# A two-layer hybrid attention trunk: ScalarE's square roots moved ahead of its first gate activations

## The chip, the core and the metric

The kernel runs on one core of a Trainium2 chip. The metric is the device time of one execution in microseconds (us). TensorE (PE) multiplies matrices, VectorE (DVE) and ScalarE (ACT) work element by element, SyncE (SP) and GpSimd (POOL) start the transfers. Each engine works through its own queue in order; semaphores order the engines against each other. ScalarE evaluates functions from a table that it holds; where the function of an instruction is not in it, the program has an ACT_TABLE_LOAD ahead of that instruction. Copy, Identity, Square and Relu show no load here; Tanh and Sqrt each show one after the other.

## What is computed

Two layers over 256 tokens of width 1024, in float32. What matters here is the token mixer:

```python
proj = jnp.einsum('bsd,dn->bsn', h, w_in)
cq, ckv, kr, qkv_b, qkv_c, iq, ik, iw, gate_logits = split_columns(proj)
q_a = jnp.einsum('bsr,rn->bsn', rms_norm(cq, g_cq), w_uq).reshape(B, S, MLA_HEADS, MLA_QK)
kv_a = jnp.einsum('bsr,rn->bsn', rms_norm(ckv, g_ckv), w_ukv).reshape(B, S, MLA_HEADS, MLA_NOPE + MLA_V)
...
q_a = rms_norm(q_a, qn_mla).transpose(0, 2, 1, 3)
k_a = rms_norm(k_a, kn_mla).transpose(0, 2, 1, 3)
q_a = jnp.concatenate([q_a[..., :MLA_NOPE], apply_rope(q_a[..., MLA_NOPE:], pos)], axis=-1)
...
g_a, g_b, g_c = jnp.split(jax.nn.sigmoid(gate_logits), 3, axis=-1)
merged = g_a * y_a + g_b * y_b + g_c * y_c
return jnp.einsum('bsd,de->bse', merged, w_out)
```

Branch a is latent attention (8 heads of 96), branches b and c have 4 heads of 64 each with normalized q and k ("pairs"), and c has an indexer of 16 small heads. Every rms_norm needs a sum of squares, a square root and a reciprocal. Before the mixer stands a modulated rms_norm, after it a second one with a SwiGLU.

## The kernel before, in words

**Slabs.** All weights stream through a ring of three slabs, up to 128 x 2048 floats. SP loads slab n into `raw` when VectorE is done with slab n-3. ScalarE copies it rounded into `w_hi` (`hi(l, s)`, L873), VectorE subtracts to get the rest `w_lo` (`lo(l, s)`, L1174), and TensorE multiplies three times per tile (hi x hi, lo x hi, hi x lo; L479 to 481 for gate slabs, L542 to 544 for the latents' slabs). `hi` waits for its transfer and until TensorE has used slab n-3; `lo` waits for `hi`; TensorE waits for `lo`. There is no planner: each engine's order is written out by hand.

**Slabs around the change**, in TensorE's order: GATE0 and GATE0+1 (gates 0 and 1), UQ, UQ+1, UQ+2 (latents to q, 128 x 1536), UKV (latents to k and v, inside the indexer's heads), GATE1 to GATE1+5 (gates 2 to 7). A gate is a slab product in a bank of PSUM that `gate_act` (L918) turns by Tanh with scale 0.5 (sigmoid written through tanh), with a signal `gate_out`.

**ScalarE, first place** (L982 to L1028): slab UQ, squares of the latents (L992), the latents turned and scaled (L997), gate 0, slab UQ+1, squares of the c pairs (L1003), the two roots of the latents (L1009), gate 1, slab UQ+2, squares of the b pairs, the two roots of the pairs (L1017), slabs UKV and GATE1, the copies of q out of PSUM (L1026), then 16 relus of the indexer (L1046) with the squares of q (L1033), slab GATE1+1 and the copies of k and v (L1040) among them, slab GATE1+2, copies of the pairs (L1051). TensorE waits for both gates (L641) before the indexer's first score (L651, L652), since those go into the gates' banks.

**VectorE, first place**: lo of UQ, the rest of the latents (L1285), lo of UQ+1, a tile of the modulation (L1181, twice), the sums of the c pairs (L1293), the reciprocal, the rotary key (L1306 to L1313), lo of UQ+2, another tile, the sums of the b pairs, the normalization of the c pairs, lo of UKV, then the indexer's sums (L1344, L1346) behind each relu.

**Second place.** ScalarE (L1055 to L1066): squares of k, root 1 for q's heads (L1057), gate 2, slab GATE1+3, root 2 for k's heads (L1063), and gates 3 to 5, each with a slab behind it. VectorE (L1377 to L1414): lo of GATE1+2, the head sums of q (L1380), the gain on q (L1384), q's rotation (L1388 to L1393), the head sums of k (L1396, L1399), lo of GATE1+3, then the norms of q and k. The signal `mss_done` goes from the head sums to the roots, `mstd_done` back.

Of the kernel before, what the change touches and what calls it, by code (L numbers as in the profile page):

```python
# [9 lines left out]
ALU = mybir.AluOpType  # L10
ACT = mybir.ActivationFunctionType
AX_X = mybir.AxisListType.X

P = 128
# [4 lines left out]
TT = T // P  # L19
# [4 lines left out]
A_HEADS, A_NOPE, A_ROPE, A_QK, A_V = 8, 64, 32, 96, 64  # L24
# [123 lines left out]
def slab_words(s):  # L148

    if S_B <= s < S_GATE0:  # L150
        return PB
    return 2 * Q_RANK if S_UQ <= s < S_UKV else SLAB


def gate_slab_no(g):

    return S_GATE0 + g if g < 2 else S_GATE1 + g - 2


def gate_bank(g):  # L160

    return 7 - g if g < 2 else g % 3 if g < 6 else g % 2
# [32 lines left out]
def build(nc, x, c, ada, slabs, vec, gain_rows, const, out):  # L195
    with ExitStack() as ctx:
        def sb(name, shape, dt=F32):
            return ctx.enter_context(nc.sbuf_tensor(name, shape, dt))

        def event(name, per_layer):  # L200
            return Event(ctx.enter_context(nc.semaphore(name)), per_layer)
# [12 lines left out]
        acc = sb("acc", [P, 3072])  # L214
# [13 lines left out]
        eps = small[:, 0:1]  # L228
        ssc = small[:, 1:5]
        krss = small[:, 5:7]  # L230
# [8 lines left out]
        ss16b = small[:, 48:64]  # L239
# [38 lines left out]
        def gate(g):  # L278
            if g < 6:
                at = [C_IQ, 1024, C_C][g // 2]  # L280
                return proj[:, g % 2, at:at + 512]
            return own[:, (g - 6) * 512:(g - 5) * 512]
# [61 lines left out]
        msq_done = event("msq_done", 2)  # L344
        mss_done = event("mss_done", 2)
        mstd_done = event("mstd_done", 2)
# [510 lines left out]
        def _(act):  # L857
            nc.scalar.dma_start(cols[:, :, :].rearrange("p l r -> p (l r)"), vec).then_inc(vec_in.sem, 16)
            nc.scalar.dma_start(konst[:, 0:P], const[:, 0:P]).then_inc(ident_in.sem, 16)
            link = Chain(act, act_chain)  # L860
# [5 lines left out]
            def hi(l, s):  # L866

                n, w = l * NS + s, slab_words(s)
                act.wait_ge(raw_in[n % RING].sem, 16 * (n // RING + 1))
                if n >= RING:  # L870

                    act.wait_ge(slab_used.sem, n - RING + 1)
                nc.scalar.activation(w_hi[:, n % RING, 0:w], raw[:, n % RING, 0:w], ACT.Copy).then_inc(hi_ready.sem, 1)  # L873
# [44 lines left out]
            def gate_act(l, g):  # L918

                s = gate_slab_no(g)  # L920
                act.wait_ge(slab_used.sem, slab_used.at(l, s + 1))
                nc.scalar.activation(gate(g), bank[gate_bank(g)][:, :], ACT.Tanh, scale=0.5).then_inc(gate_out.sem, 1)
# [17 lines left out]
            for l in range(DEPTH):  # L940
# [55 lines left out]
                for k in range(KT):  # L996
                    nc.scalar.activation(y_hi[:, k, :], bank[k // 2][:, (k % 2) * T:(k % 2 + 1) * T], ACT.Copy,  # L997
                                         scale=cols[:, l, R_GQ + k:R_GQ + k + 1]).then_inc(cq_hi.sem, 1)
                gate_act(l, 0)
                hi(l, S_UQ + 1)  # L1000

                def pair_squares(kind, base):
# [5 lines left out]
                for m, n in ((0, Q_RANK), (1, KV_RANK)):  # L1008
                    nc.scalar.activation(ssc[:, 2 * m:2 * m + 2], ssc[:, 2 * m:2 * m + 2], ACT.Sqrt, bias=eps,  # L1009
                                         scale=1.0 / n).then_inc(cq_std.sem, 1)  # L1010
                gate_act(l, 1)
                hi(l, S_UQ + 2)
                act.wait_ge(pss_done.sem, pss_done.at(l, 1))
                pair_squares(1, C_B)
                for kind, ss in ((0, ss16), (1, ss16b)):
                    act.wait_ge(pss_done.sem, pss_done.at(l, kind + 1))
                    nc.scalar.activation(ss, ss, ACT.Sqrt, bias=eps, scale=1.0 / HD).then_inc(pstd_done.sem, 1)  # L1017
                hi(l, S_UKV)
                hi(l, S_GATE1)

                act.wait_ge(cq_rstd.sem, cq_rstd.at(l, 1))
                act.wait_ge(slab_used.sem, slab_used.at(l, S_UQ + 3))
                for t in range(TT):
                    for ch in range(2):
                        at = t * Q_RANK + 384 * ch
                        nc.scalar.activation(q_a[:, at:at + 384], bank[2 * t + ch][:, 0:384], ACT.Copy,  # L1026
                                             scale=ssc[:, t:t + 1]).then_inc(uq_out.sem, 1)
# [28 lines left out]
                                     ACT.Square).then_inc(msq_done.sem, 1)  # L1056
                nc.scalar.activation(ss16, ss16, ACT.Sqrt, bias=eps, scale=1.0 / A_QK).then_inc(mstd_done.sem, 1)  # L1057

                act.wait_ge(kr_done.sem, kr_done.at(l, 1))
                gate_act(l, 2)  # L1060
                hi(l, S_GATE1 + 3)
                act.wait_ge(mss_done.sem, mss_done.at(l, 2))
                nc.scalar.activation(ss16b, ss16b, ACT.Sqrt, bias=eps, scale=1.0 / A_QK).then_inc(mstd_done.sem, 1)  # L1063
                for g in range(3, 6):
                    gate_act(l, g)
                    hi(l, S_GATE1 + g + 1)  # L1066
                for kind in range(2):
                    act.wait_ge(mla_tp.sem, mla_tp.at(l, kind + 1))
                    for b in range(2):
                        m = A_HEADS * kind + 2 * b  # L1070
# [87 lines left out]
        def _(dve):  # L1158
            link = Chain(dve, dve_chain)
# [10 lines left out]
            def lo(l, s):  # L1170

                n, w = l * NS + s, slab_words(s)
                dve.wait_ge(hi_ready.sem, n + 1)
                nc.vector.tensor_tensor(w_lo[:, n % RING, 0:w], raw[:, n % RING, 0:w], w_hi[:, n % RING, 0:w],  # L1174
                                        ALU.subtract).then_inc(lo_ready.sem, 1)
# [58 lines left out]
            for l in range(DEPTH):  # L1234
# [131 lines left out]
                def k_rows(kind):  # L1366

                    dve.wait_ge(pair_tp.sem, pair_tp.at(l, kind + 1))
                    for e in range(2):
# [12 lines left out]
                qv = q_a.rearrange("p (m d) -> p m d", d=A_QK)  # L1382
                q4 = q_a.rearrange("p (t h d) -> p t h d", t=TT, h=A_HEADS)
                link(nc.vector.tensor_tensor(qv, qv, gains[:, 0:A_QK].unsqueeze(1).to_broadcast([P, 16, A_QK]), ALU.mult))  # L1384
                rot = q4[:, :, :, A_NOPE:A_QK]
                ra = acc[:, 1536:2048].rearrange("p (t h d) -> p t h d", t=TT, h=A_HEADS)
                rb = acc[:, 2048:2560].rearrange("p (t h d) -> p t h d", t=TT, h=A_HEADS)
# [4 lines left out]
                                             .to_broadcast([P, TT, A_HEADS, half]), ALU.mult))  # L1392
                link(nc.vector.tensor_tensor(rot, ra, rb, ALU.add))  # L1393

                dve.wait_ge(msq_done.sem, msq_done.at(l, 2))
                link(nc.vector.tensor_reduce(ss16b, acc[:, 0:1024].rearrange("p (m d) -> p m d", d=A_NOPE), AX_X,  # L1396
                                             ALU.add))
                sb3 = ss16b.rearrange("p (t h) -> p t h", t=TT)
                nc.vector.tensor_tensor(sb3, sb3, krss.unsqueeze(2).to_broadcast([P, TT, A_HEADS]), ALU.add)\  # L1399
                    .then_inc(mss_done.sem, 1)  # L1400
                lo(l, S_GATE1 + 3)
                dve.wait_ge(mstd_done.sem, mstd_done.at(l, 1))
                link(nc.vector.reciprocal(ss16, ss16))
# [15 lines left out]
                for kind in range(2):  # L1419
                    dve.wait_ge(mla_tp.sem, mla_tp.at(l, kind + 1))  # L1420
                    for b in range(2, 4):
                        m = A_HEADS * kind + 2 * b
# [234 lines left out]
```

## Time and profile before

| | us |
|---|---|
| median of 3 runs | 994.08 (994.02 to 995.42) |
| profiled execution | 991.47 |
| its span | 989.3 |
| TensorE busy | 935.7 (95%) |
| VectorE busy | 694.0 (70%) |
| ScalarE busy | 482.7 (49%) |

The span runs from the first to the last instruction that the profile shows; the profiled execution's own time has 2.2 us around it. Times in the rows are counted from the start of the span. "L922" is line 922 of the kernel; a tile's name stands without its number. In a row of a time line, the brackets give how long the engine stood idle before it and which instruction ended that. Consecutive instructions of an engine overlap by about 0.1 us in the rows, so that start plus duration may lie just behind the next start.

### The profile page before, as it was taken

To read this page: it belongs to the slowest core of one execution; us is meant where nothing else is said; L and a number is where in the kernel's file an instruction comes from. 1 tells how busy PE (TensorE), PEld (TensorE's weight loads), DVE (VectorE), ACT (ScalarE), POOL (GpSimd) and SP (SyncE) were. 2 spreads that over 40 slices of the span, in tenths; PEclk is the share of its full clock that TensorE was granted. 3 is DMA by queue.
4 is the path that set the end of the run, shared out by engine and by line. 5 is a ranking of instruction groups with operands and counts; after the bars stand their busy time and mean duration, and the time that the engine had idled before them with its cause. 6 is when DMAs were issued, how large, how long until landed. Compare 5 with 4: busy or idle time off the path is not lost.

```text
span 989.3 us, 15954 instructions
## 1 busy us (share of the span) xinstructions
PE 935.7 (95%) x6744; PEld 880.1 (89%) x6744; DVE 694.0 (70%) x1087; ACT 482.7 (49%) x654; POOL 24.4 (2%) x49
## 2 busy tenths in 40 slices
PE   8998989998998999999989998999989899999998
PEld 6787969976987999999978997898779799999998
DVE  4997889787784656666574797988878555656443
ACT  4554776455445433343463468374553454333341
POOL 1010000000000000000000000000000000000000
PEclk8999999999998999999989999999999789999999
DMA  9979633414652776767545795251454434654541
GB/s 361 384 285 373 238 114 132 171 44 171 255 213 86 256 255 216 280 237 281 181 170 183 273 327 187 92 204 45 172 211 173 171 128 171 218 207 172 178 164 43
DMA packets 29593, 198.31 MB, mean 200 GB/s; under 512 B 3282, under 2 KB 3794, under 8 KB 7507
## 3 DMA queue, kind: packets, MB, share of 16 engines
q1 hardware_dynamic: 23474, 155.22, 43.6%
q0 software_dynamic: 5760, 41.95, 11.5%
q8 instruction: 53, 0.87, 0.3%
q10 hardware_dynamic: 288, 0.14, 0.0%
q14 instruction: 18, 0.14, 0.0%
HBM read 196.24 MB, written 1.05 MB: 199 GB/s over the span
## 4 chain that ended last, share of the span: by engine, by line
PE 62%; DVE 24%; ACT 7%; issue 4%; DMA 3%; ACTq 0%; DVEq 0%
PE bank L479 16%; PE bank L481 16%; PE bank L480 16%; DVE w_lo L1174 7%; ACT w_hi L873 2%; DVE front L1181 2%; DVE score L1346 2%; DMA raw<-in_slabs_dram 2%; DVE acc L1437 2%; PE bank L506 1%; PE bank L586 1%; PE bank L585 1%; PE bank L587 1%; DVE score L1364 1%; ACT acc L1083 1%
## 5 line engine op out<-in xcount | busy, mean ns | idle before, releaser
L1174 DVE TENSOR_TENSOR w_lo<-raw,w_hi 128x2048 fp32r<-128x2048 f32 (+2 forms) x146 | 314.6, 2160 | 138.7 <-ACT w_hi L873 137.1
L479 PE MATMUL bank<-h_hi,w_hi 128*128 128x256 f32 x1216 | 350.8, 289 | 12.1 <-DVE w_lo L1174 6.2
L873 ACT ACTIVATE w_hi<-raw 128x2048 fp32r<-128x2048 f32 (+2 forms) x146 | 262.9, 1806 | 175.0 <-PE bank L481 120.9
L481 PE MATMUL bank<-h_hi,w_lo 128*128 128x256 f32 x1216 | 347.2, 286 | 0.0
L480 PE MATMUL bank<-h_lo,w_hi 128*128 128x256 f32 x1216 | 347.2, 285 | 0.0
L479 PEld LDWEIGHTS bank<-h_hi,w_hi 128*128 128x128 f32 x1216 | 236.5, 194 | 16.7 <-issue 14.9
L480 PEld LDWEIGHTS bank<-h_lo,w_hi 128*128 128x128 f32 x1216 | 236.5, 195 | 0.1
L481 PEld LDWEIGHTS bank<-h_hi,w_lo 128*128 128x128 f32 x1216 | 236.4, 194 | 0.0
L479 PE MATMUL bank<-y_hi,w_hi 128*128 128x256 f32 x480 | 135.6, 282 | 2.2 <-DVE w_lo L1174 2.2
L480 PE MATMUL bank<-y_lo,w_hi 128*128 128x256 f32 x480 | 135.1, 282 | 0.0
L481 PE MATMUL bank<-y_hi,w_lo 128*128 128x256 f32 x480 | 135.0, 281 | 0.0
L479 PEld LDWEIGHTS bank<-y_hi,w_hi 128*128 128x128 f32 x480 | 90.4, 188 | 2.9 <-DVE w_lo L1174 2.6
L1181 DVE CUSTOM_DVE_ANT_0 front<-front,cond,cols 128x1024 f32<-128x1024 f32 x72 | 89.5, 1280 | 4.2 <-DMA front<-in_ada_dram 4.2
L480 PEld LDWEIGHTS bank<-y_lo,w_hi 128*128 128x128 f32 x480 | 90.4, 188 | 0.0
L481 PEld LDWEIGHTS bank<-y_hi,w_lo 128*128 128x128 f32 x480 | 90.3, 188 | 0.0
L1132 ACT ACTIVATE proj<-bank 128x512 f32<-128x512 f32 x22 | 13.1, 595 | 87.2 <-PE bank L481 87.2
L1083 ACT ACTIVATE acc<-acc,small 128x128 f32<-128x128 f32 x64 | 28.6, 449 | 45.1 <-DVE small L1441 45.0
L1528 DVE TENSOR_TENSOR proj<-proj,bank 128x512 f32<-128x512 f32 x22 | 15.1, 687 | 50.5 <-ACT proj L1132 50.5
L585 PE MATMUL bank<-w_hi,h_hi 128*128 128x512 f32 x112 | 43.9, 392 | 1.9 <-DVE h_lo L1222 1.9
L587 PE MATMUL bank<-w_lo,h_hi 128*128 128x512 f32 x112 | 43.6, 390 | 0.0
L586 PE MATMUL bank<-w_hi,h_lo 128*128 128x512 f32 x112 | 43.6, 389 | 0.0
L437 POOL DMA_DIRECT2D front<-in_ada_dram x31 | 16.5, 534 | 746.5 <-DVE mod L1181 464.2
(171 smaller groups left out, 1151.2 us busy)
## 6 DMA issues: line engine op xcount, KB each, us to landing
raw<-in_slabs_dram SPq DMA_DIRECT2D x124, 1024.0 KB, 5.1
front<-in_ada_dram POOLq DMA_DIRECT2D x31, 1024.0 KB, 5.7
acc<-in_ada_dram POOLq DMA_DIRECT2D x9, 1024.0 KB, 5.7
raw<-in_slabs_dram SPq DMA_DIRECT2D x16, 552.0 KB, 4.9
front<-in_ada_dram SPq DMA_DIRECT2D x5, 1024.0 KB, 11.4
raw<-in_slabs_dram SPq DMA_DIRECT2D x6, 768.0 KB, 6.7
proj<-in_ada_dram SPq DMA_DIRECT2D x2, 1024.0 KB, 9.1
x_t<-in_x_dram SPq DMA_DIRECT2D x2, 512.0 KB, 5.3
```

The costliest lines, as they stand in the source:

```text
L479: nc.tensor.matmul(b_out, st_hi, mv_hi, start=start, stop=False, skip_group_check=True)
L480: nc.tensor.matmul(b_out, st_hi, mv_lo, start=False, stop=False, skip_group_check=True)
L481: return nc.tensor.matmul(b_out, st_lo, mv_hi, start=False, stop=stop, skip_group_check=True)
L585: nc.tensor.matmul(o, hh, wh, start=False, stop=False)
L586: nc.tensor.matmul(o, hl, wh, start=False, stop=False)
L587: last = nc.tensor.matmul(o, hh, wl, start=False, stop=(k == KT - 1))
L873: nc.scalar.activation(w_hi[:, n % RING, 0:w], raw[:, n % RING, 0:w], ACT.Copy).then_inc(hi_ready.sem, 1)
L1083: nc.scalar.activation(p_sb[n % 4][:, c0:c1], p_sb[n % 4][:, c0:c1], ACT.Exp, bias=negmax[n % 2][:, t:t + 1], scale=slope, accum_out=rowsu ...
L1174: nc.vector.tensor_tensor(w_lo[:, n % RING, 0:w], raw[:, n % RING, 0:w], w_hi[:, n % RING, 0:w], ALU.subtract).then_inc(lo_ready.sem, 1)
L1181: ins = nc.vector.tensor_tensor_reduce(w, w, cond[:], 1.0, cols[:, l, col:col + 1], ALU.mult, ALU.add, mod[:, l, col:col + 1])
L1346: ins = nc.vector.scalar_tensor_tensor(out=score[:, c0:c1], in0=relu_b[h % 4][:, c0:c1], scalar=wt, in1=score[:, c0:c1], op0=ALU.mult, op1 ...
L1437: nc.vector.tensor_tensor_reduce(p_sb[n % 4][:, c0:c1], bank[4 + n % 2][:, c0:c1], mask[:, c0:c1], 1.0, NEG, ALU.add, ALU.max, rowmax[n % ...
```

## The change

ScalarE does gates 0 and 1 only behind the roots of the latents and of the pairs, between slabs UKV and GATE1, and root 2 of the latent branch's heads ahead of gate 2. For that, VectorE makes the head sums of k ahead of q's rotation and not behind it. No instruction of arithmetic is added or removed; table loads are placed by the program's build ahead of what needs them.

```diff
@@ ScalarE
                     nc.scalar.activation(y_hi[:, k, :], bank[k // 2][:, (k % 2) * T:(k % 2 + 1) * T], ACT.Copy,
                                          scale=cols[:, l, R_GQ + k:R_GQ + k + 1]).then_inc(cq_hi.sem, 1)
-                gate_act(l, 0)
                 hi(l, S_UQ + 1)
...
                     nc.scalar.activation(ssc[:, 2 * m:2 * m + 2], ssc[:, 2 * m:2 * m + 2], ACT.Sqrt, bias=eps,
                                          scale=1.0 / n).then_inc(cq_std.sem, 1)
-                gate_act(l, 1)
                 hi(l, S_UQ + 2)
...
                     nc.scalar.activation(ss, ss, ACT.Sqrt, bias=eps, scale=1.0 / HD).then_inc(pstd_done.sem, 1)
                 hi(l, S_UKV)
+                gate_act(l, 0)
+                gate_act(l, 1)
                 hi(l, S_GATE1)
...
                 nc.scalar.activation(ss16, ss16, ACT.Sqrt, bias=eps, scale=1.0 / A_QK).then_inc(mstd_done.sem, 1)
 
+                act.wait_ge(mss_done.sem, mss_done.at(l, 2))
+                nc.scalar.activation(ss16b, ss16b, ACT.Sqrt, bias=eps, scale=1.0 / A_QK).then_inc(mstd_done.sem, 1)
                 act.wait_ge(kr_done.sem, kr_done.at(l, 1))
                 gate_act(l, 2)
                 hi(l, S_GATE1 + 3)
-                act.wait_ge(mss_done.sem, mss_done.at(l, 2))
-                nc.scalar.activation(ss16b, ss16b, ACT.Sqrt, bias=eps, scale=1.0 / A_QK).then_inc(mstd_done.sem, 1)
                 for g in range(3, 6):
@@ VectorE
                 link(nc.vector.tensor_tensor(qv, qv, gains[:, 0:A_QK].unsqueeze(1).to_broadcast([P, 16, A_QK]), ALU.mult))
+                dve.wait_ge(msq_done.sem, msq_done.at(l, 2))
+                link(nc.vector.tensor_reduce(ss16b, acc[:, 0:1024].rearrange("p (m d) -> p m d", d=A_NOPE), AX_X,
+                                             ALU.add))
+                sb3 = ss16b.rearrange("p (t h) -> p t h", t=TT)
+                nc.vector.tensor_tensor(sb3, sb3, krss.unsqueeze(2).to_broadcast([P, TT, A_HEADS]), ALU.add)\
+                    .then_inc(mss_done.sem, 1)
                 rot = q4[:, :, :, A_NOPE:A_QK]
...
                 link(nc.vector.tensor_tensor(rot, ra, rb, ALU.add))
 
-                dve.wait_ge(msq_done.sem, msq_done.at(l, 2))
-                link(nc.vector.tensor_reduce(ss16b, acc[:, 0:1024].rearrange("p (m d) -> p m d", d=A_NOPE), AX_X,
-                                             ALU.add))
-                sb3 = ss16b.rearrange("p (t h) -> p t h", t=TT)
-                nc.vector.tensor_tensor(sb3, sb3, krss.unsqueeze(2).to_broadcast([P, TT, A_HEADS]), ALU.add)\
-                    .then_inc(mss_done.sem, 1)
                 lo(l, S_GATE1 + 3)
```

## Rows read from the trace of the kernel before

**Rows 1.** The page, busy time of an engine, share of the span, instructions.

```profile
PE 935.7 (95%) x6744; PEld 880.1 (89%) x6744; DVE 694.0 (70%) x1087; ACT 482.7 (49%) x654; POOL 24.4 (2%) x49
```

**Rows 2.** ScalarE's groups by form: line, operation, count, busy us, mean ns, idle before.

```profile
L922 ACT ACT_TABLE_LOAD x8 | 10.3, 1283 | 0.1
...
L1009 ACT ACT_TABLE_LOAD x2 | 2.6, 1283 | 0.0
L1017 ACT ACT_TABLE_LOAD x2 | 2.6, 1283 | 0.0
L1063 ACT ACT_TABLE_LOAD x2 | 2.6, 1283 | 0.0
```

**Rows 3.** TensorE's time line at its stalls: start, us, instruction, idle before and releaser.

```profile
97.19 0.36 PE L479 MATMUL bank<-h_hi,w_hi 128*128 128x256 f32 x1 [3.23 <-DVE w_lo L1174]
...
131.39 0.49 PE L651 MATMUL bank<-ikz,front 128*128 128x128 f32 x2 [2.77 <-ACT acc L1046]
...
168.13 0.39 PE L479 MATMUL bank<-h_hi,w_hi 128*128 128x256 f32 x1 [0.53 <-DVE w_lo L1174]
...
496.01 0.39 PE L479 MATMUL bank<-y_hi,w_hi 128*128 128x256 f32 x1 [1.72 <-DVE w_lo L1174]
...
650.40 0.39 PE L479 MATMUL bank<-h_hi,w_hi 128*128 128x256 f32 x1 [0.52 <-DVE w_lo L1174]
```

**Rows 4.** ScalarE's time line at the first place, layer 0.

```profile
106.45 3.03 ACT L997 ACTIVATE y_hi<-bank,cols 128x256 fp32r<-128x256 f32 x8 [2.98 <-PE bank L631]
109.50 1.28 ACT L922 ACT_TABLE_LOAD   x1
...
111.29 1.48 ACT L873 ACTIVATE w_hi<-raw 128x1536 fp32r<-128x1536 f32 x1
...
125.02 0.31 ACT L1017 ACTIVATE small<-small 128x16 f32<-128x16 f32 x1 [3.66 <-DVE small L1293]
125.23 3.69 ACT L873 ACTIVATE w_hi<-raw 128x2048 fp32r<-128x2048 f32 x2
128.84 1.97 ACT L1026 ACTIVATE front<-bank,small 128x384 f32<-128x384 f32 x4
```

**Rows 5.** VectorE's time line at the first place, layer 0.

```profile
99.37 2.29 DVE L1174 TENSOR_TENSOR w_lo<-raw,w_hi 128x2048 fp32r<-128x2048 f32 x1
...
107.33 3.23 DVE L1285 SCALAR_TENSOR_TENSOR y_lo<-bank,cols,y_hi 128x256 fp32r<-128x256 f32 x8 [1.58 <-ACT y_hi L997]
112.80 1.76 DVE L1174 TENSOR_TENSOR w_lo<-raw,w_hi 128x1536 fp32r<-128x1536 f32 x1 [2.25 <-ACT w_hi L873]
...
136.06 3.30 DVE L1346 SCALAR_TENSOR_TENSOR score<-acc,proj,score 128x128 f32<-128x128 f32 x8 [1.58 <-ACT acc L1046]
```

**Rows 6.** Windows: length, busy time by engine, TensorE's granted clock, DMA share, GB/s.

```profile
98.30:101.70 3.40, 3.40 (x18) 3.40 (x17) 3.40 (x4) 3.40 (x7) 0.53 (x1) 0.50 0.76 244
136.10:168.10 32.00, 30.16 (x216) 27.84 (x214) 30.63 (x47) 16.96 (x26) 0.00 (x0) 1.00 0.29 99
```

**Rows 7.** ScalarE's time line at the second place, layer 0.

```profile
161.68 0.29 ACT L1057 ACTIVATE small<-small 128x16 f32<-128x16 f32 x1
...
163.28 0.60 ACT L922 ACTIVATE proj<-bank 128x512 f32<-128x512 f32 x1
163.77 1.91 ACT L873 ACTIVATE w_hi<-raw 128x2048 fp32r<-128x2048 f32 x1
```

**Rows 8.** VectorE's time line at the second place, layer 0.

```profile
162.32 0.69 DVE L1388 TENSOR_TENSOR acc<-front,konst 128x512 f32<-128x512 f32 x1
...
164.44 1.22 DVE L1396 TENSOR_REDUCE small<-acc 128x16 f32<-128x1024 f32 x1
165.69 0.17 DVE L1399 TENSOR_TENSOR small<-small 128x16 f32<-128x16 f32 x1
165.79 2.28 DVE L1174 TENSOR_TENSOR w_lo<-raw,w_hi 128x2048 fp32r<-128x2048 f32 x1
```

**Rows 9.** The page's DMA issues: queue, count, KB each, median us to landing.

```profile
raw<-in_slabs_dram SPq DMA_DIRECT2D x6, 768.0 KB, 6.7
```

## The prediction, made before the change was run

> **What bounds the kernel now.** I read the page first: TensorE is busy 95% of the span, VectorE 70%, ScalarE 49% [rows 1]. So ScalarE's busy time as such is free, and what counts is where another engine stands still behind it. Next the groups of ScalarE by form, for the table loads: 8 ahead of the tanh of `gate_act` (L922), 2 each ahead of the roots of L1009, L1017 and L1063, each 1283 ns [rows 2]. That is 7 a layer in the part that the change touches (the 7 others, of line 864, lie outside). Then the time lines of ScalarE, VectorE and TensorE around the two places of the diff, in layer 0. Layer 1 runs the same pattern 482.27 us later (650.40 less 168.13 [rows 3]), so each term counts twice.
>
> *First place, 106 to 136 us.* ScalarE turns the latents (L997) until 109.48, loads a table, takes gate 0, and begins the high part of slab UQ+1 at 111.29 [rows 4]. VectorE has long finished its own part (107.33 + 3.23 = 110.56) and waits 2.25 us for that slab, until 112.80 [rows 5]. From there its queue is full until the sums of the second pair, for which ScalarE waits 3.66 us, until 125.02 [rows 4]. After that ScalarE is the late one: root, two slabs (125.23), the four copies of line 1026 (128.84), the first relus; TensorE waits 2.77 us for the first relu, until 131.39 [rows 3, 4], and VectorE takes up the indexer's sums 4 to 7 at 136.06, again behind ScalarE [rows 5].
>
> *Second place, 136 to 190 us.* VectorE is busy 30.63 of 32.00 us from 136.1 to 168.1 [rows 6], its gaps are those between chained instructions, and TensorE waits 0.53 us for its low part of slab GATE1+3, until 168.13 [rows 3]. So whatever delays VectorE's queue before 168.13 delays TensorE there by the same, and whatever comes early on TensorE or ScalarE gains nothing. ScalarE has its high part of that slab ready early: 163.77 + 1.91 = 165.68 [rows 7], against VectorE's start at 165.79 [rows 8]. That is 0.1 us of cover, and the change spends it.
>
> **The change, first place (gates 0 and 1 moved behind the pair roots).** Removed ahead of UQ+1: a load and a tanh. The slab begins at 109.38 (it overlaps the end of L997 by the 0.1 us that a slab overlaps any ScalarE predecessor [rows 4]) and not at 111.29: 1.91 us earlier. VectorE is free at 110.56 and the slab is ready at 110.86, so VectorE gains 1.91 - about 110.9 for 112.80. The roots of the latents need no load any more, nor do the pair roots, since the table of roots is still in place. UQ+2 begins behind UQ+1 (1.48 - 0.1), the squares (1.05) and the two roots (0.48), at 112.3. Its data are asked for when VectorE is done with the slab three before, at 99.37 + 2.29 = 101.66 [rows 5], and such a load takes 6.7 us [rows 9]: there at 108.4, in time. VectorE's queue holds nothing else that waits, so the pair sums end 1.91 earlier too, and the last pair root starts at 125.02 - 1.91 = 123.11.
>
> Added behind slab UKV and ahead of slab GATE1: one load (1.28, and 0.1 of overlap lost as the load waits for the slab to end), gate 0 and gate 1 at about 0.5 each as they overlap (0.60 alone). That is 2.40 with the gaps of 0.01 to 0.02. Queued behind it on ScalarE are GATE1, the copies of line 1026 and the first relus, and for these both other engines stand still. So the copies begin at 128.84 - 1.91 + 2.40 = 129.33: **0.5 us later**. TensorE's first score now also waits for both gates, until 127.6; that is 1.7 before it would matter. The term is +0.5 a layer. The relus, VectorE's sums and its whole full queue up to 168 shift with it, so it is not given back.
>
> **Second place.** VectorE makes the second head sum before the rotation. Its sum of 1.22 and addition of 0.17 now start at 162.32, where the rotation did, and end at 162.32 + (165.69 - 164.44) + 0.17 = 163.74 [rows 8]; the squares that they need are there (ScalarE's root behind them starts at 161.68 [rows 7]). The rotation follows and ends at 165.8 as the whole did. The work is the same, so this alone costs nothing. On ScalarE, root 1 now needs a load, since the tanh of gates 0 and 1 came before it: 161.68 + 1.30 + 0.3 = 163.3, still ahead of 163.8, hidden with 0.5 us to spare. Root 2 waits for the sum, 163.82 to 164.13. Then come the load (1.28) and gate 2, at 165.44 and not at 163.28: 2.16 later [rows 7]. Slab GATE1+3 is queued behind gate 2 and ends at 165.68 + 2.16 = 167.84. VectorE is ready for it at 165.79 and starts at 167.87. So VectorE waits **2.1 us** where it waited for nothing, and TensorE gets the slab at 170.2, not 168.13. The two loads that disappear behind this point (L1063's and the next of L922) lay after the slab and hid behind gate slabs on TensorE; their removal gives nothing. Later TensorE runs without a stall until the scores, so the 2.1 is not made up.
>
> Table loads per layer: 7 become 3 (gate 0, root 1, gate 2), 10.3 us of ScalarE in all, and none of it from the chain except the 1.91 above.
>
> **The clock.** TensorE's stall at 168.13 grows from 0.53 to 2.6 us. The stalls of 3.23 and 2.77 us [rows 3] were each followed by 3.4 us at a granted clock of 0.50, that is 1.2 GHz and not 2.4, the first of the two in [rows 6]; the one of 1.72 us at 496.01 [rows 3] was not. A new 2.6 lies between them. At half clock 3.4 us of slab work loses 1.7 us, and here TensorE is what everybody waits for. Bounds 0 and 1.7 a layer. Nearest in size is 2.77, but there the engine also had only short matmuls around the stall, so I take 0.7, a little under half.
>
> **The sum.** (0.5 + 2.1 + 0.7) x 2 = 6.6 us. The profiled execution took 991.47 (span 989.3), the median of the runs is 994.08: 998.1 for a profiled execution like that one, **1000.6 for the median**. Without any fall of the clock it would be 999.3, with one in each layer 1002.7.
>
> **A rule on the other side.** The rows show a switch of tables as 1.30 us, load to activation. The Trainium skill ("ScalarE: Activation LUTs", Table sets: the hidden batching unit) says to batch activations by set, all of one set before switching, which is just what this change does; a reader of the rule alone would expect a gain. The same page (What ACT_TABLE_LOAD costs) counts another 1.38 us of drain with each load, 2.66 in all. By that price root 1 would come after the sum and add some 0.9 a layer, an estimate from the page; no row here shows the drain.
>
> **Rivals.** (1) *The batching pays.* If the two gates at their new place are covered, because TensorE or VectorE and not ScalarE decides when line 1026 begins, and if slab GATE1+3 is not waited for, then what is left is the 1.91 a layer that VectorE gets early: 994.1 - 3.8 = 990.3. It decides from 0.5 us on: the gates must hide that much of their 2.40. Against it: ScalarE has no gap from 125.02 through the relus, and TensorE waits for it. (2) *The second wait is hidden.* If VectorE's rotation is slower in its new place, or slab GATE1+3 comes before gate 2's tanh could hold it up, only the first term is left: 995.1. Against it: one queue, in order. (3) *The clock falls in both layers*: 1002.7. (4) *The low clock of 132 to 136 goes*, as the first scores now run later and break the stall in two. It lost 1.7 a layer on TensorE, but VectorE's queue is full there; if TensorE did decide, 999.3 - 3.4 = 995.9. (5) *It doesn't do what it says*: the loads stay 7 a layer, ScalarE would be slower still, about 1002.
>
> **Chances.** Forecast with 0 to one fall of the clock 0.63, (3) 0.19, (5) 0.02, (2) and (4) together 0.09, (1) 0.07. The range runs from just over (4) to just over (3): 996.0 to 1003.2; outside lie (1), (2) and the edges. About 0.2% (2.0 us) is what a measurement of this kernel tells from no change: slower by more 0.85, within 0.08, faster 0.07.
>
> **What would show it.** Right: 13 table loads in all, for 21; VectorE's low part of UQ+1 at about 110.9; line 1026 at 129.3; a new idle of about 2 us of VectorE ahead of a low part, ended by ScalarE, near 168; TensorE's stall there 2.6. Wrong at the first term: TensorE's stall at 131 doesn't move. Wrong at the second: slab GATE1+3's high part ends before VectorE's rotation. Wrong in size: clock falls of another number than one.

## The result, and the profile of the changed kernel

The changed kernel takes 998.97 us (median of 18 runs), the kernel before 994.00 in the same comparison (18 runs): a ratio of 1.0051, 95% interval 1.0036 to 1.0066, or +5.1 us (3.6 to 6.6). The forecast was +6.6, and +5.2 without its term for the clock. Single runs of one kernel differ by several us, so below the sizes are read from distances inside one trace, and the ratios only say whether these carry through to the end.

The page of the changed kernel and its table loads (line, operation, count, busy us, mean ns, idle before):

```profile
PE 940.2 (94%) x6744; PEld 883.9 (89%) x6744; DVE 693.9 (70%) x1087; ACT 472.5 (47%) x646; POOL 24.3 (2%) x49
```

```profile
L922 ACT ACT_TABLE_LOAD x4 | 5.1, 1283 | 0.1
L1057 ACT ACT_TABLE_LOAD x2 | 2.6, 1283 | 0.0
```

ScalarE is busy 10.2 us less than in [rows 1]: 6 loads in this part and not 14 [rows 2]. The kernel is slower all the same.

ScalarE's time line in the changed kernel, layer 0, first and second place:

```profile
107.07 3.02 ACT L997 ACTIVATE y_hi<-bank,cols 128x256 fp32r<-128x256 f32 x8 [3.95 <-PE bank L631]
109.94 1.54 ACT L873 ACTIVATE w_hi<-raw 128x1536 fp32r<-128x1536 f32 x1
...
123.72 0.31 ACT L1015 ACTIVATE small<-small 128x16 f32<-128x16 f32 x1 [5.63 <-DVE small L1293]
123.94 1.90 ACT L873 ACTIVATE w_hi<-raw 128x2048 fp32r<-128x2048 f32 x1
125.86 1.28 ACT L922 ACT_TABLE_LOAD   x1
127.15 1.09 ACT L922 ACTIVATE proj<-bank 128x512 f32<-128x512 f32 x2
128.12 1.91 ACT L873 ACTIVATE w_hi<-raw 128x2048 fp32r<-128x2048 f32 x1
129.92 2.00 ACT L1026 ACTIVATE front<-bank,small 128x384 f32<-128x384 f32 x4
...
162.90 1.28 ACT L1057 ACT_TABLE_LOAD   x1
164.20 0.31 ACT L1057 ACTIVATE small<-small 128x16 f32<-128x16 f32 x1
164.88 0.31 ACT L1060 ACTIVATE small<-small 128x16 f32<-128x16 f32 x1 [0.38 <-DVE small L1389]
165.21 1.28 ACT L922 ACT_TABLE_LOAD   x1
166.51 0.60 ACT L922 ACTIVATE proj<-bank 128x512 f32<-128x512 f32 x1
167.00 1.91 ACT L873 ACTIVATE w_hi<-raw 128x2048 fp32r<-128x2048 f32 x1
```

From the end of line 997 (107.07 + 3.02 = 110.09) to line 1026 it is 19.83 us, against 128.84 - 109.48 = 19.36 in [rows 4]: +0.47. ScalarE now waits 5.63 us for the second pair sums where it waited 3.66; the gates stand behind that wait, where nothing hides them. At the second place root 1 has its load, root 2 waits 0.38 for VectorE, and gate 2 and the slab come behind it.

VectorE and TensorE behind it, at the second place; the first row is that of the head sums of q in the kernel before, the others are of the changed kernel:

```profile
158.87 1.75 DVE L1380 TENSOR_REDUCE small<-acc 128x16 f32<-128x1536 f32 x1
```

```profile
159.98 1.75 DVE L1380 TENSOR_REDUCE small<-acc 128x16 f32<-128x1536 f32 x1
...
169.01 2.29 DVE L1174 TENSOR_TENSOR w_lo<-raw,w_hi 128x2048 fp32r<-128x2048 f32 x1 [2.16 <-ACT w_hi L873]
```

```profile
171.36 0.39 PE L479 MATMUL bank<-h_hi,w_hi 128*128 128x256 f32 x1 [1.04 <-DVE w_lo L1174]
```

The row of 165.79 in [rows 8] had no idle time; here VectorE waits 2.16 us. From the head sums of q to that low part it is 169.01 - 159.98 = 9.03 us, against 165.79 - 158.87 = 6.92 before: +2.11. TensorE gets the slab 3.23 later than the 168.13 of [rows 3], 0.61 of which was already there at line 997. Its own stall is 1.04 and not the 2.6 forecast, for it was late itself. These are its two stalls ahead of that, and its stall ahead of the first scores in layer 1; then two windows, one behind the second of these stalls and one over the first scores of layer 1 (length, busy times by engine, granted clock, DMA share, GB/s):

```profile
128.29 0.38 PE L651 MATMUL bank<-ikz,front 128*128 128x128 f32 x1 [2.84 <-ACT proj L922]
...
149.48 0.33 PE L661 MATMUL bank<-konst,proj 128*128 128x128 f32 x1 [2.47 <-ACT acc L1046]
...
615.29 0.58 PE L651 MATMUL bank<-ikz,front 128*128 128x128 f32 x1 [3.60 <-ACT proj L922]
```

```profile
150.30:153.50 3.20, 3.20 (x17) 3.20 (x16) 2.90 (x7) 2.01 (x3) 0.00 (x0) 0.50 0.38 100
614.50:621.10 6.60, 5.81 (x19) 5.09 (x20) 2.77 (x6) 5.96 (x11) 0.00 (x0) 0.50 0.44 159
```

The second of these stalls, ahead of the transposes of the pairs, was in the kernel before:

```profile
148.37 0.33 PE L661 MATMUL bank<-konst,proj 128*128 128x128 f32 x1 [1.07 <-ACT acc L1046]
```

The first scores wait for the gates (the releaser is the tanh, L922). The low clock (0.50, 1.2 GHz) that lay at 132.4 to 135.8 has moved: in layer 0 a stretch of 3.4 us begins at 129.7, behind the stall and over the short matmuls of the first scores, and a second one at 150.2, in gate slab GATE1, where VectorE's coming wait of 2.16 us leaves TensorE time to lose it in. In layer 1 the stretch over the first scores lasts 6.8 us (614.4 to 621.2), the relus wait for the scores, and the fifth relu comes late (idle of VectorE before its sums 4 to 7 2.32, against 1.58 in [rows 5]):

```profile
624.89 1.20 DVE L1346 SCALAR_TENSOR_TENSOR score<-acc,proj,score 128x128 f32<-128x128 f32 x3 [2.32 <-ACT acc L1046]
```

That is +0.74 us in this layer. Summed from the trace: layer 0 0.47 + 2.11, layer 1 0.46 + 0.74 + 2.11, together 5.9 us. The profiled execution took 999.65 (span 997.5) against 991.47 (span 989.3); the other 2.3 us lie outside the two places, in stretches of low clock and in the time of layer 0's line 997, and differ from run to run.

### The profile page after: what moved, and what is told of

Read it like the earlier page. It is cut to its first block, busy times and chain, and to the rows that moved or that the text cites. A ratio compares the mean times of both kernels' runs of the same rounds, so it can differ in the third digit from the quotient of the medians.

```text
span 997.5 us, 15948 instructions
## 1 busy us (share of the span) xinstructions
PE 940.2 (94%) x6744; PEld 883.9 (89%) x6744; DVE 693.9 (70%) x1087; ACT 472.5 (47%) x646; POOL 24.3 (2%) x49
## 4 chain that ended last, share of the span: by engine, by line
PE 58%; DVE 25%; ACT 8%; issue 4%; DMA 3%; ACTq 0%; DVEq 0%
PE bank L479 16%; PE bank L481 16%; PE bank L480 16%; DVE w_lo L1174 7%; DVE front L1181 3%; ACT w_hi L873 3%; DMA raw<-in_slabs_dram 3%; DVE score L1346 2%; DVE acc L1437 2%; PE bank L585 1%; PE bank L587 1%; PE bank L586 1%; PE bank L506 1%; DVE score L1364 1%; ACT acc L1083 1%
```

## The experiments

The distances given below are taken in each trace for layer 0 / layer 1: A, from the end of line 997 to line 1026; B, VectorE's idle ahead of the low part of GATE1+3. Before: A 19.36 / 19.36, B 0 / 0. The change: A 19.83 / 19.82, B 2.16 / 2.15. A ratio is the time over that of the kernel before, with its 95% interval; 0.0010 of it is 1.0 us.

**The first place alone.**

```diff
-                gate_act(l, 0)
                 hi(l, S_UQ + 1)
...
-                gate_act(l, 1)
                 hi(l, S_UQ + 2)
...
                 hi(l, S_UKV)
+                gate_act(l, 0)
+                gate_act(l, 1)
                 hi(l, S_GATE1)
```

> The first place of the change alone: gates 0 and 1 behind the pair roots, root 2 left behind slab GATE1+3. Queue theory (ScalarE's order decides, the wait is passed on at full length): +0.5 us a layer at the first place, since the gates' 2.4 outweigh the 1.9 that VectorE gains; and at the second place root 1 now needs a table load, so that slab GATE1+3 ends 1.3 late against 0.1 of cover: VectorE waits 1.2 ahead of that slab's low part. In all +1.7 a layer, +3.4 us over before. Rival (batching pays: 5 loads a layer and not 7 take time off): faster than before, by up to 3.8. Rival (only the clock counts): as the change itself, +5, with new stretches of low clock.

Measured: ratio 1.0050 (1.0027 to 1.0074), A 19.81 / 19.82, B 1.26 / 1.27. Its time lines at the second place:

```profile
162.11 1.28 ACT L1057 ACT_TABLE_LOAD   x1
163.41 0.31 ACT L1057 ACTIVATE small<-small 128x16 f32<-128x16 f32 x1
163.73 1.28 ACT L922 ACT_TABLE_LOAD   x1
165.03 0.60 ACT L922 ACTIVATE proj<-bank 128x512 f32<-128x512 f32 x1
165.52 1.90 ACT L873 ACTIVATE w_hi<-raw 128x2048 fp32r<-128x2048 f32 x1
```

```profile
167.46 2.29 DVE L1174 TENSOR_TENSOR w_lo<-raw,w_hi 128x2048 fp32r<-128x2048 f32 x1 [1.26 <-ACT w_hi L873]
```

Moving the gates leaves the tanh table in place at root 1, and the load that this brings, some 37 us further on, is passed to VectorE in full. Both distances are as the queue has it; batching saved two loads a layer and no time. The ratio holds the expected 1.0034 inside its interval. The clock did here what it does in layer 0 of the change: TensorE waits 2.83 us for the gates ahead of the first scores, stalls 2.54 / 2.67 us ahead of the pairs' transposes, and low clock lies from 149.2 and from 637.3, 3.4 us each. So this goes with the gates' new place and not with the second place.

**The second place alone.**

```diff
                 nc.scalar.activation(ss16, ss16, ACT.Sqrt, bias=eps, scale=1.0 / A_QK).then_inc(mstd_done.sem, 1)
 
+                act.wait_ge(mss_done.sem, mss_done.at(l, 2))
+                nc.scalar.activation(ss16b, ss16b, ACT.Sqrt, bias=eps, scale=1.0 / A_QK).then_inc(mstd_done.sem, 1)
                 act.wait_ge(kr_done.sem, kr_done.at(l, 1))
                 gate_act(l, 2)
                 hi(l, S_GATE1 + 3)
-                act.wait_ge(mss_done.sem, mss_done.at(l, 2))
-                nc.scalar.activation(ss16b, ss16b, ACT.Sqrt, bias=eps, scale=1.0 / A_QK).then_inc(mstd_done.sem, 1)
```

(with VectorE's head sums of k ahead of the rotation, as in the change)

> The second place alone: VectorE's head sums of k ahead of the rotation, root 2 ahead of gate 2; gates 0 and 1 as in the kernel before. Queue theory: root 2 waits for the sum until 163.8, so gate 2 and slab GATE1+3 come 2.1 us late and VectorE waits 2.1: +4.2 us for two layers, with 5 loads a layer. The two parts don't add (3.4 + 4.2 against 5.1 measured for both), because the load ahead of root 1 that costs 1.2 when alone hides behind the wait for the sum. Rival (batching pays): no slower than before. Rival (the sum ahead of the rotation itself costs VectorE time): VectorE's instructions longer, its idle ahead of the slab unchanged.

Measured: ratio 1.0055 (1.0034 to 1.0077), A 19.36 / 19.36, B 2.15 / 2.15. VectorE's row, TensorE's two rows, and a window behind each of these stalls:

```profile
170.79 2.29 DVE L1174 TENSOR_TENSOR w_lo<-raw,w_hi 128x2048 fp32r<-128x2048 f32 x1 [2.15 <-ACT w_hi L873]
```

```profile
173.13 0.39 PE L479 MATMUL bank<-h_hi,w_hi 128*128 128x256 f32 x1 [2.64 <-DVE w_lo L1174]
...
659.69 0.39 PE L479 MATMUL bank<-h_hi,w_hi 128*128 128x256 f32 x1 [2.63 <-DVE w_lo L1174]
```

```profile
660.50:663.70 3.20, 3.20 (x17) 3.20 (x16) 3.13 (x4) 1.31 (x1) 0.00 (x0) 0.50 0.93 310
173.20:176.60 3.40, 3.40 (x29) 3.40 (x30) 3.30 (x5) 2.06 (x2) 0.00 (x0) 1.00 0.76 222
```

With TensorE on time, its stall is the 2.6 us of the forecast. Of two such stalls one was followed by 1.2 GHz (0.50) and one was not (1.00). Where it was, from the low part of the slab to the attention scores it took 24.68 us and not 23.34: 1.3 us. That was the forecast's third term, in the kernel for which it holds. Each part alone has a ratio that can't be told from that of the whole change. By the distances they are 1.8 us a layer (0.46 at the first place, and the low part 1.34 later behind the head sums of q) and 2.1, and together 2.6: they don't add, since the load ahead of root 1 hides behind root 2's wait once both are in. In this run's trace the end of line 997 in layer 0 is at 112.39 and not at 109.48: 2.9 us of its time lie ahead of anything that was edited, where the matmuls of line 506, from 10.5 us on, came every 0.21 us and not every 0.11 as before, which is half the rate. So this execution's own time overstates the edit.

**Gates 0 and 1 where ScalarE has nothing to do.**

```diff
                 for kind, ss in ((0, ss16), (1, ss16b)):
+                    if kind == 1:
+                        gate_act(l, 0)
+                        gate_act(l, 1)
+                        table(ACT.Sqrt)
                     act.wait_ge(pss_done.sem, pss_done.at(l, kind + 1))
```

(the two gates taken out ahead of UQ+1 and UQ+2; the rest as in the kernel before)

> The kernel before with gates 0 and 1 between the two pair roots, where ScalarE waits for the second sums (5.6 us in the changed kernel), and the table of roots loaded again behind them; second place as before, loads 5 a layer plus one. Queue theory: the 1.9 us that VectorE gains at slab UQ+1 stay, and the gates are covered by ScalarE's own idle time: line 1026 begins 1.9 us earlier than in before, and -1.9 a layer, -3.8 us in all, about 990.2. Root 1 has its table, so nothing changes at the second place. Rival (clock): the stall of TensorE ahead of the first relu stays near 2.8, its fall of the clock too, same as before within 1 us. Rival (TensorE becomes the bound once ScalarE is early): -1 us or less.

Measured: ratio 0.9974 (0.9951 to 0.9998), A 17.50 / 17.50, B 0 / 0. ScalarE's time line:

```profile
117.43 1.28 ACT L922 ACT_TABLE_LOAD   x1
118.72 1.09 ACT L922 ACTIVATE proj<-bank 128x512 f32<-128x512 f32 x2
119.83 1.28 ACT L864 ACT_TABLE_LOAD   x1
121.12 0.20 ACT L864 ACTIVATE small<-small 128x1 f32<-128x1 f32 x1
123.10 0.31 ACT L1019 ACTIVATE small<-small 128x16 f32<-128x16 f32 x1 [1.77 <-DVE small L1295]
...
126.92 1.97 ACT L1028 ACTIVATE front<-bank,small 128x384 f32<-128x384 f32 x4
```

(L1019 is the roots' line here, L1028 is line 1026 of the kernel before.) Two loads and two gates stand in the idle time, of which 1.77 us are left, and A is 1.86 shorter than before in each layer. So the gain that the first edit set free was real; the gates' new place had taken it back. The expected 0.9962 lies inside the interval, and the interval ends just below 1: that the kernel is faster is shown, but only just.

**The change with slab GATE1+3 first.**

```diff
+                hi(l, S_GATE1 + 3)
                 act.wait_ge(mss_done.sem, mss_done.at(l, 2))
                 nc.scalar.activation(ss16b, ss16b, ACT.Sqrt, bias=eps, scale=1.0 / A_QK).then_inc(mstd_done.sem, 1)
                 act.wait_ge(kr_done.sem, kr_done.at(l, 1))
                 gate_act(l, 2)
-                hi(l, S_GATE1 + 3)
```

> The whole change, but slab GATE1+3 goes ahead of root 2 and gate 2 on ScalarE; 3 loads a layer as in the change. Queue theory: the slab is ready at 165.2 to 165.7 on the old time line, VectorE no longer waits for it, gate 2 comes at about 167.4, still ahead of TensorE's need of its bank at 168.1. The second term goes, the first (0.5 a layer) stays: +1.0 us over before, about 995. Rival (the sum's new place on VectorE costs): stays at +4 or more. Rival (gate 2 is now too late for gate 5): TensorE stalls for a tanh near 168 by up to 1 us a layer.

Measured: ratio 1.0035 (1.0004 to 1.0066), A 19.83 / 19.82, B 0 / 0. VectorE's low part of GATE1+3, and a window in GATE1's slab in layer 0:

```profile
167.17 2.29 DVE L1174 TENSOR_TENSOR w_lo<-raw,w_hi 128x2048 fp32r<-128x2048 f32 x1
```

```profile
150.60:154.00 3.40, 3.40 (x18) 3.40 (x17) 3.09 (x8) 2.00 (x3) 0.00 (x0) 0.50 0.50 145
```

The second term is gone and the sum's new place costs VectorE nothing: from the head sums of q to the low part it is 6.91 us. The low clock of layer 0 again fell into GATE1's slab (150.6 to 154.0), and now there was no wait to lose it in: from the low part of GATE1+3 to the attention scores it took 24.02 us in layer 0, against 23.33 in layer 1, where no such stretch lay. In layer 1 the first scores wait for the gates as in the change (3.59 us), but the low clock behind that stall lasts 3.4 us and not 6.8, and the fifth relu is not late (1.59). The ratio is above the expected 1.0010, with an interval that still holds it.

**Both places mended.** The edits of the last two experiments together.

> Both places mended: gates 0 and 1 between the two pair roots (table of roots loaded again behind them), VectorE's head sums of k ahead of the rotation, and slab GATE1+3 ahead of root 2 and gate 2. 3 table loads a layer: gate 0, pair root, gate 2. Queue theory: as the kernel with the gates in the gap, which has 5 loads a layer: line 1026 begins 17.5 us behind the end of line 997 (19.36 in before), no wait ahead of the low part of GATE1+3; -3.8 us over before, and nothing more for the 4 loads fewer. Rival (loads have a price of their own): another 5.2 us less than the kernel with 5 loads.

Measured: ratio 0.9965 (0.9947 to 0.9982), A 17.50 / 17.51, B 0 / 0. Its loads, and then those of the kernel with the gates in the gap:

```profile
L864 ACT ACT_TABLE_LOAD x9 | 11.5, 1283 | 1.8 <-PEq L1642 1.6
L922 ACT ACT_TABLE_LOAD x4 | 5.1, 1283 | 0.1
```

```profile
L864 ACT ACT_TABLE_LOAD x9 | 11.5, 1283 | 1.8 <-PEq L1642 1.6
L922 ACT ACT_TABLE_LOAD x6 | 7.7, 1283 | 0.1
L1065 ACT ACT_TABLE_LOAD x2 | 2.6, 1283 | 0.0
```

Four loads fewer, 5.1 us of ScalarE, and the distances are the same; the ratios agree within their intervals, and a price of 5.2 us for the four loads would have taken the ratio below this interval. 989.7 us is the lowest median of this study, though the times don't tell it from the kernel with the gates in the gap. Line 1026 comes 1.86 us a layer earlier, 3.7 in all, which is 0.9963 and so as much as the measured gain.

**A load behind or ahead of the slab.** The first try was one line, `table(ACT.Silu)`, behind root 2 and then ahead of gate 2.

> The kernel before with one more load a layer, of a table that nothing uses (1.28, with a tiny activation some 1.5 us), between root 2 and gate 3, behind slab GATE1+3. Queue theory: 0.0, as ScalarE is some 2.4 us early there (slab GATE1+4 is ready at 171.0, VectorE takes it at 173.4). Rival (each load costs time wherever it stands): +3.0 us.

> The kernel before with the same additional load a layer, but ahead of gate 2 and so of slab GATE1+3. Queue theory: the slab is late by 1.5 less 0.1 of cover: VectorE's idle ahead of its low part 1.4, +2.8 us for two layers. Together with the run that has it behind the slab: same load, other place. Rival (load priced by number): the same for both.

Measured: ratios 1.0005 (0.9984 to 1.0027) and 1.0005 (0.9985 to 1.0024). The dose was not given. The load that Silu brought serves the tanh behind it too, and it replaced that load. With it ahead of gate 2, one activation of 0.20 us was all that was added (21 loads, as before), and the low part of GATE1+3 came 7.08 us behind the head sums of q and not 6.92: 0.16 of the 0.20 us is passed on. With it behind root 2 there are 23 loads, but the additional one a layer stands elsewhere than meant: the exponential of the attention scores, which needs no load behind the tanh in the kernel before, needs one behind Silu's table:

```profile
189.86 1.28 ACT L1084 ACT_TABLE_LOAD   x1
```

ScalarE stood idle for 0.94 us ahead of that instruction before, and neither the distances of the slabs behind it nor the ratio show the load. The next two give the dose with a pair.

```diff
+                table(ACT.Tanh)
+                table(ACT.Sqrt)
                 gate_act(l, 2)
                 hi(l, S_GATE1 + 3)
```

> The kernel before with two more table loads a layer that change nothing (a tanh of one column, then a root of one column: 2 x 1.3 and 2 x 0.2, about 3.0 us), ahead of gate 2 and so of slab GATE1+3. The single activation tried before brought no load with it, only its 0.2 us. Queue theory: VectorE's idle ahead of the low part of GATE1+3 is 3.0 less 0.1 of cover, 2.9 a layer, +5.8 us for two layers. Rival (ScalarE is at half load and absorbs it): 0.

Measured: ratio 1.0102 (1.0084 to 1.0121), B 2.87 / 2.87. VectorE, TensorE and a window behind:

```profile
171.48 2.29 DVE L1176 TENSOR_TENSOR w_lo<-raw,w_hi 128x2048 fp32r<-128x2048 f32 x1 [2.87 <-ACT w_hi L873]
```

```profile
173.83 0.58 PE L479 MATMUL bank<-h_hi,w_hi 128*128 128x256 f32 x1 [3.48 <-DVE w_lo L1176]
```

```profile
174.00:179.00 5.00, 5.00 (x24) 5.00 (x25) 4.90 (x6) 4.99 (x5) 0.00 (x0) 0.50 0.64 213
```

The wait is as expected. The ratio is 10.1 us (8.3 to 12.0), more than the 5.8 of the waits alone: in TensorE's stall of 3.48 a stretch of 6.8 us at 1.2 GHz began (172.5 to 179.3), through most of the slab, and from the low part to the scores it took 25.60 us and not 23.34, 2.3 more in this layer. Layer 1 lost none there (23.34); its stall was 1.89. What the rest of the difference was, this run doesn't settle: in its trace, too, line 997 of layer 0 ends 2.75 us late, at 112.23, ahead of anything that was edited.

```diff
                 nc.scalar.activation(ss16b, ss16b, ACT.Sqrt, bias=eps, scale=1.0 / A_QK).then_inc(mstd_done.sem, 1)
+                table(ACT.Tanh)
+                table(ACT.Sqrt)
                 for g in range(3, 6):
```

> The kernel before with the same two loads a layer, but behind root 2, where slab GATE1+3 is done. Queue theory: of the 3.0 us some 2.4 are covered; the low part of GATE1+4 comes 0.6 late on VectorE and TensorE sees at most 0.5 a layer, 0 to +1.0 us in all. Rival (loads are priced by number): as with the pair ahead of gate 2, +5.8.

Measured: ratio 1.0003 (0.9986 to 1.0020), B 0 / 0.

```profile
177.23 0.39 PE L479 MATMUL bank<-h_hi,w_hi 128*128 128x256 f32 x1 [0.54 <-DVE w_lo L1176]
```

The same pair, one slab later: a stall of 0.54 us on TensorE and 0.8 us a layer up to the scores, a little over the 0.5 expected, together 1.6 us, which the times can't tell from zero. One place costs 1% and the other at most 0.2%.

**TensorE kept busy**, on top of both places mended.

```diff
+                pe.wait_ge(ukv_out.sem, ukv_out.at(l, 4))
+                for _ in range(5):
+                    nc.tensor.matmul(bank[0][:, 0:T], kz_t[:, 0, 0:P], kz_t[:, 0, :], start=True, stop=True)
                 pe.wait_ge(relu_done.sem, relu_done.at(l, IDX_HEADS))
```

> Both places mended as above, and TensorE does 5 additional matmuls a layer into a free bank (a product that nothing reads) in its stall ahead of the transposes of the pairs. Clock theory: in the changed kernel the stall there grew from 1.06 to 2.2 to 2.5 us and a stretch of 3.4 us at 1.2 GHz then lay in the gate slabs behind it; with the additional work there is no such stretch in 150 to 154 nor 638 to 642, and up to 0.8 us a layer less than without it wherever it fell. Rival (TensorE's clock there costs nothing, VectorE decides): the same time within 1 us, whether or not the stretch is there.

Measured: ratio 0.9968 (0.9944 to 0.9993), A 17.51 / 17.50. The stall ahead of the pairs' transposes is gone, and no low clock lies behind it; but none lay there in the trace without the additional work either, although its stall was 2.76 us in layer 0 (1.07 in layer 1). The experiment had nothing to mend and is inconclusive.

**The change once more.**

> The change once more, unaltered, for a second trace of it. Expected whatever the clock does: 19.8 us from the end of line 997 to line 1026, and 2.15 us of VectorE's idle ahead of the low part of GATE1+3, in both layers; ratio about 1.005. Clock theory of the prediction (a fall behind the longer stall ahead of GATE1+3 costs 1.7): a stretch at 1.2 GHz within 6 us behind that stall in about one layer of two. Rival (TensorE comes late to that stall, since it stood and ran slow earlier, so the stall stays near 1): no such stretch, low clock at 150 and 638 instead.

Measured: ratio 1.0051 (1.0033 to 1.0068), A 19.84 / 19.82, B 2.15 / 2.15; TensorE's stall ahead of GATE1+3 1.28 / 1.04, with no low clock behind it; low clock from 127.7, 148.1 and 636.2, 3.4 us each, and 6.8 us from 612.3, where VectorE again stands idle 2.31 us before its sums 4 to 7. The second trace repeats the first in both distances, in the stalls and in where the low clock lies.

## Why the prediction was right, and where it was off

*First term, +0.5 a layer.* Measured +0.47 and +0.46, against 0.49 in the forecast's working. The steps hold: UQ+1 starts right behind line 997, VectorE's queue and the pair sums move up by 1.9, load and two gates put 2.4 behind slab UKV. That ScalarE decides line 1026 is shown from the other side by the gates in the gap, where A falls by 1.86.

*Second term, +2.1 a layer.* Measured 2.11. That it is the order on ScalarE, and not the sum's new place on VectorE, is shown by the kernel with the slab first, where it vanishes; and by the second place alone, where it stands without the first. The load at root 1 was hidden as stated, with 164.20 + 0.31 = 164.51 against root 2's start at 164.88, 0.37 to spare and not 0.5.

*Third term, the clock, 0.7 a layer.* This step failed: in its place, and by half in its size. The forecast took TensorE's stall ahead of GATE1+3 to grow to 2.6 us, as if TensorE were on time. It was not: the first scores wait for the gates, the low clock over the scores comes earlier, the stall ahead of the pairs' transposes grew from 1.07 to 2.47 (layer 1: 1.06 to 2.17), and a stretch of 1.2 GHz fell into slab GATE1. So the stall was 1.04 to 1.28, with no fall behind it, in both traces of the change. What the clock did cost is 0.74 in layer 1, at the first scores, where the forecast had said that their wait for the gates was 1.7 us from mattering. With 3.4 us of half clock over the scores that holds (layer 0, where nothing was lost); with 6.8 us it doesn't. The stall of 2.6 and its fall in one layer of two, for 1.3 us, exist where the second place is changed alone. Why a stretch lasts 3.4 us in one place and 6.8 in another stays open.

*The sum.* 6.6 forecast, 5.1 (3.6 to 6.6) measured, 5.9 by the distances in the trace. (994.08 + 6.6 is 1000.7 and not the 1000.6 that was written.) The two terms of the queues, 5.2, are in the middle of the interval; the third term was mis-sized: 0.4 a layer on average and not 0.7. The times alone can't tell the three sums apart, so that term is known from the traces only. The 0.7 stood for a fall that did not come, and another one came where the forecast had seen none; that the sum is near all the same is luck in this term.

*Rivals.* Batching pays: no. 8 loads fewer gave back nothing as placed, 4 loads fewer between the two mended kernels gave nothing either, and 4 loads more a kernel cost 10.1 us in one place and in the other nothing that the times show (1.6 by the distances). The second wait hidden: no. Low clock in both layers behind the stall: not in the change. The low clock of 132 to 136 did move, and no time was won by it: from line 1026 to the head sums of q it is 30.04 us before and 30.06 in layer 0 of the change. The loads fell to 13, so the change does what it says.

*The Trainium skill.* Its price of a switch with a drain (2.66 us, "ScalarE: Activation LUTs", What ACT_TABLE_LOAD costs) is not what these traces show: from load to activation 1.30 us, as in 162.90 to 164.20, with the load starting 0.01 to 0.03 us behind the instruction before it. Its rule to batch by set (same page, Table sets: the hidden batching unit) did take away loads, 21 to 13, and 10.2 us of ScalarE's busy time; here that was not the bound.

## What to carry to other kernels

A table load cost here what stood behind it in its queue: count the loads that another engine waits for, not the loads. Before moving work away from one wait, look for the idle time of the same engine that can take it; 5.6 us were there, a few instructions ahead of where the gates were put. And when an order changes the table that is left in place, follow it to the next function that needs another one, however far: here some 37 us on.

## What the runs showed of the hardware that was not expected

The low clock moves with the stalls. TensorE's stalls of 2.2 to 2.8 us ahead of gate slabs were followed by 3.4 us at 1.2 GHz in some places and not in others, in the same program: 2.63 with and 2.64 without in the two layers of the kernel with the second place alone, 2.75 with and 2.75 without in the kernel with the slab first, 2.17 with in layer 1 of the change. What decides between them no run here shows.

A stretch of low clock costs its 1.7 us (half of 3.4) only where TensorE decides. In the kernel before it was lost at the indexer: where it lies there, TensorE's stall ahead of the pairs' transposes is 1.07 us, and where none lies there (layer 1 of the second place alone, layer 0 of both places mended) that stall is 2.76, 1.7 longer, at the same distance from line 1026 to the head sums of q. In the change it was lost in a wait that came later; in the kernel without that wait 0.7 of it came through.
